# Long attention on one core: two score halves issued in turns, value column halves alternating, PSUM banks reassigned

## What is computed

```python
q = q.reshape(B, S, G, R, dh).transpose(0, 2, 3, 1, 4) * dh ** -0.5      # G=4 groups, R=4 heads each, dh=64
sc = jnp.where(vis, jnp.einsum('bgrqd,bgnd->bgrqn', qb, k_cmp), NEG)     # 15 compressed keys
o_cmp = jnp.einsum('bgrqn,bgnd->bgrqd', p_cmp, v_cmp)
sc = jnp.einsum('bgrqd,bgqkd->bgrqk', qb, ksel)                          # selected keys, causal
o_slc = jnp.einsum('bgrqk,bgqkd->bgrqd', jax.nn.softmax(sc, axis=-1), vsel)
sc = jnp.where(wmask, jnp.einsum('bgrqd,bgkd->bgrqk', qb, kwin), NEG)    # window keys, causal
o_win = jnp.einsum('bgrqk,bgkd->bgrqd', jax.nn.softmax(sc, axis=-1), vwin)
return gb[..., 0:1] * o_cmp + gb[..., 1:2] * o_slc + gb[..., 2:3] * o_win
```

## Time and profile before

| | us |
|---|---|
| median of 3 runs | 1858.64 (1858.28 to 1859.43) |
| the profiled execution, its own time | 1860.6 |
| its span, first to last instruction | 1858.7 |
| TensorE busy in it | 1715.8 (92%) |
| VectorE busy | 1038.0 (56%) |
| ScalarE busy | 791.7 (43%) |
| mean granted TensorE clock | 0.954 of full |

### The profile page before, as it was taken

One profiled execution on the slowest core, in us unless ns is written; L12 is line 12 of the kernel. 1 busy time (PEld: TensorE's weight loads), 2 busy tenths in 40 slices (PEclk: granted clock), 3 DMA queues, 4 the chain that ended last, 5 costly groups with the idle time before them and its releaser, 6 DMA issues.

```text
span 1858.7 us, 22342 instructions
## 1 busy us (share of the span) xinstructions
PE 1715.8 (92%) x8605; PEld 1414.5 (76%) x8605; DVE 1038.0 (56%) x1326; ACT 791.7 (43%) x963; POOL 96.7 (5%) x143
## 2 busy tenths in 40 slices
PE   6999978899999999989898989999899887789996
PEld 6788867688888788889855777888688673668885
DVE  4577654466655676645554435555548653655553
ACT  4434433365434444333455335555444433334441
POOL 1000000010000000010000003000100010200000
PEclk8999989999999999999899999999899895799998
DMA  8687734177864677633400425556365330536550
GB/s 288 201 277 262 233 108 157 40 255 252 268 226 147 229 259 262 225 104 101 167 33 1 139 69 174 190 189 213 108 231 204 109 106 1 170 125 203 181 181 23
DMA packets 210195, 311.74 MB, mean 168 GB/s; under 512 B 16537, under 2 KB 145589, under 8 KB 209872
## 3 DMA queue, kind: packets, MB, share of 16 engines
q1 hardware_dynamic: 204112, 288.90, 46.6%
q0 software_dynamic: 6016, 21.94, 3.4%
HBM read 306.59 MB, written 4.21 MB: 167 GB/s over the span
## 4 chain that ended last, share of the span: by engine, by line
PE 85%; DVE 6%; ACT 3%; issue 3%; DMA 1%; PEld 1%; POOL 1%; DVEq 0%; PEldq 0%; ACTq 0%; SPq 0%; POOLq 0%
PE ps L1994 24%; PE ps L1996 24%; PE ps L1995 24%; DVE wlo L1304 1%; PE ps L2035 1%; PE ps L2330 1%; PE ps L2116 1%; PE ps L2217 1%; PE ps L2315 1%; DMA area<-in_gate_b 1%; PE ps L2045 1%; PE ps L2198 1%; PE ps L2418 1%; PE ps L2306 1%; ACT xn L811 0%
## 5 line engine op out<-in xcount | busy, mean ns | idle before, releaser
L1304 DVE TENSOR_TENSOR wlo<-raw,whi 128x2048 fp32r<-128x2048 f32 x255 | 581.0, 2298 | 238.1 <-ACT whi L757 237.3
L757 ACT ACTIVATE whi<-raw 128x2048 fp32r<-128x2048 f32 x255 | 481.2, 1910 | 207.1 <-PE ps L1996 183.7
L1994 PE MATMUL ps<-wlo,aT_hi 128*128 128x512 f32 (+1 forms) x1280 | 500.2, 391 | 22.1 <-DVE aT_lo L1330 9.2
L1996 PE MATMUL ps<-whi,aT_hi 128*128 128x512 f32 (+1 forms) x1280 | 493.4, 385 | 0.0
L1995 PE MATMUL ps<-whi,aT_lo 128*128 128x512 f32 (+1 forms) x1280 | 493.0, 385 | 0.0
L1994 PEld LDWEIGHTS ps<-wlo,aT_hi 128*128 128x128 f32 x1280 | 244.1, 191 | 72.6 <-issue 15.0
L1996 PEld LDWEIGHTS ps<-whi,aT_hi 128*128 128x128 f32 x1280 | 243.5, 190 | 47.9
L1995 PEld LDWEIGHTS ps<-whi,aT_lo 128*128 128x128 f32 x1280 | 244.2, 191 | 45.1
L1994 PE MATMUL ps<-wlo,hT_hi 128*128 128x512 f32 x480 | 188.0, 392 | 5.4 <-DVE hT_lo L1421 3.0
L1996 PE MATMUL ps<-whi,hT_hi 128*128 128x512 f32 x480 | 187.6, 391 | 0.0
L1995 PE MATMUL ps<-whi,hT_lo 128*128 128x512 f32 x480 | 187.3, 390 | 0.0
(11 more groups left out here) (302 smaller groups left out, 1388.4 us busy)
## 6 DMA issues: line engine op xcount, KB each, us to landing
raw<-in_ffn_w_in SPq DMA_DIRECT2D x176, 512.0 KB, 4.9
raw<-in_ffn_w_out SPq DMA_DIRECT2D x88, 512.0 KB, 4.3
raw<-in_w_ff SPq DMA_DIRECT2D x64, 512.0 KB, 4.7
raw<-in_ada_w SPq DMA_DIRECT2D x48, 512.0 KB, 5.5
raw<-in_w_in SPq DMA_DIRECT2D x48, 512.0 KB, 4.7
raw<-in_xattn_w_kv SPq DMA_DIRECT2D x32, 512.0 KB, 7.0
raw<-in_xattn_w_q SPq DMA_DIRECT2D x16, 512.0 KB, 4.8
raw<-in_xattn_w_o SPq DMA_DIRECT2D x16, 512.0 KB, 4.9
```

The costliest lines, as they stand in the source:

```text
L757: act.activation(to, of, ACT.Copy).then_inc(hi_ready[slot], 1)
L1304: dve.tensor_tensor(lo, of, hi, ALU.subtract).then_inc(lo_ready[slot], 1)
L1994: pe.matmul(o, lh, rl, start=start, stop=False, skip_group_check=True)
L1996: return pe.matmul(o, lh, rh, start=False, stop=stop, skip_group_check=True)
```

## The change

Only `nsa_attend` is edited, on all three engines for the bank numbers, and on TensorE for the order.

- Scores of two units (an even and an odd head) are issued as one `score_pair(p)`: selected keys of the even head, selected keys of the odd head, window keys of the even head, window keys of the odd head. They use four banks (u % 4) instead of three.
- `values(gi)` issues both column halves in one step, alternating half 0 and half 1 for each stationary operand, between turn(4 gi + 4) and turn(4 gi + 5). Both halves accumulate in bank 7, which alone serves all groups; so it waits for out_lo of the group directly before, not of the one before that.
- Turned probabilities move to banks 4 and 5, turn_cmp to bank 6. turn_cmp is issued after the fourth unit of a group rather than after the third.
- The score of units 2p + 4 and 2p + 5 is issued after turn(2p + 1).

The numbers of matmuls, transposes, copies and vector instructions, and their shapes, are unchanged. The core of the diff:

```diff
-                    def score(u):
-                        g, t, r = u // 8, u // 4 % 2, u % 4
-                        half, w = slice(64 * (r % 2), 64 * (r % 2) + 64), P * (t + 1)
-                        if u >= 3:
-                            pe.wait_ge(maxed, units.n + u - 2)
-                        q = qT[half, 2 * g + r // 2, t * P:(t + 1) * P]
-                        pe.matmul(ps[:, u % 3, 0:w], q, ksT[half, g, 0:w], start=True, stop=True)
-                        pe.matmul(ps[:, u % 3, w:2 * w], q, kwT[half, g, 0:w], start=True, stop=True).then_inc(scored, 1)
+                    def score_pair(p):
+                        g, t, k = p // 4, p // 2 % 2, p % 2
+                        w = P * (t + 1)
+                        if p >= 2:
+                            pe.wait_ge(maxed, units.n + 2 * p - 2)
+                        for c, keys in ((0, ksT), (w, kwT)):
+                            for e in range(2):
+                                half = slice(64 * e, 64 * e + 64)
+                                last = pe.matmul(ps[:, (2 * p + e) % 4, c:c + w], qT[half, 2 * g + k, t * P:(t + 1) * P],
+                                                 keys[half, g, 0:w], start=True, stop=True)
+                                if c:
+                                    last.then_inc(scored, 1)
...
-                    def values(gi, half):
+                    def values(gi):
...
-                        if gi >= 2:
-                            pe.wait_ge(o_kept, groups.n + gi - 1)
-                        o = ps[64 * half:64 * half + 64, 6 + gi % 2, 0:256]
-                        pe.matmul(o, vcmp[:, 64 * g:64 * g + 64], nsaPc[gi % 2][0:N_CMP, half::2, :], start=True, stop=False)
+                        if gi:
+                            pe.wait_ge(o_kept, groups.n + gi)
+                        terms = [(vcmp[:, 64 * g:64 * g + 64], nsaPc[gi % 2][0:N_CMP])]
                         for j, v in enumerate((vs, vw)):
                             for m in range(t + 1):
                                 c = P * (j * (t + 1) + m)
-                                last = pe.matmul(o, v[:, m, 64 * g:64 * g + 64], nsaP[gi % 2][:, half::2, c:c + P],
-                                                 start=False, stop=j == 1 and m == t)
-                        if half == 1:
-                            last.then_inc(pv_done, 1)
+                                terms.append((v[:, m, 64 * g:64 * g + 64], nsaP[gi % 2][:, :, c:c + P]))
+                        for n, (v, probs) in enumerate(terms):
+                            for half in range(2):
+                                last = pe.matmul(ps[64 * half:64 * half + 64, 7, 0:256], v, probs[:, half::2, :],
+                                                 start=n == 0, stop=n == len(terms) - 1, skip_group_check=True)
+                        last.then_inc(pv_done, 1)
...
-                    score(0)
-                    score(1)
-                    keep_clock(30, 5)
-                    for u in range(32):
-                        if u + 2 < 32:
-                            score(u + 2)
-                        turn(u)
-                        if u % 4 == 2:
-                            turn_cmp(u // 4)
-                        if u % 4 < 2 and u >= 4:
-                            values(u // 4 - 1, u % 4)
-                    for half in range(2):
-                        values(7, half)
+                    score_pair(0)
+                    score_pair(1)
+                    keep_clock(30, 4)
+                    for p in range(16):
+                        turn(2 * p)
+                        if p % 2 == 0 and p:
+                            values(p // 2 - 1)
+                        turn(2 * p + 1)
+                        if p % 2:
+                            turn_cmp(p // 2)
+                        if p + 2 < 16:
+                            score_pair(p + 2)
+                    values(7)
```

More of the change, by code:

```diff
@@ L1036, in keep @@
                             act.wait_ge(pv_done, groups.n + gi - 1)
-                        act.activation(nsaP[gi % 2][:, r, 0:2 * P * (t + 1)], ps[:, 3 + u % 2, 0:2 * P * (t + 1)], ACT.Copy)\
+                        act.activation(nsaP[gi % 2][:, r, 0:2 * P * (t + 1)], ps[:, 4 + u % 2, 0:2 * P * (t + 1)], ACT.Copy)\
                            .then_inc(probs_kept, 1)
@@ L1043, in out_hi @@
                         act.activation(aT_hi[:, 2 * g:2 * g + 2, t * P:(t + 1) * P],
-                                       ps[:, 6 + gi % 2, 0:256].rearrange("p (j q) -> p j q", j=2), ACT.Copy).then_inc(o_hi, 1)
+                                       ps[:, 7, 0:256].rearrange("p (j q) -> p j q", j=2), ACT.Copy).then_inc(o_hi, 1)
                     def keep_cmp(gi):
@@ L1049, in keep_cmp @@
                             act.wait_ge(pv_done, groups.n + gi - 1)
-                        act.activation(nsaPc[gi % 2][0:N_CMP], ps[0:N_CMP, 5, :].rearrange("p (r q) -> p r q", r=4), ACT.Copy)\
+                        act.activation(nsaPc[gi % 2][0:N_CMP], ps[0:N_CMP, 6, :].rearrange("p (r q) -> p r q", r=4), ACT.Copy)\
                            .then_inc(cmp_kept, 1)
@@ L1639, in top @@
                         for j in range(2):
-                            last = dve.tensor_tensor_reduce(Pb[u % 3][:, w * j:w * j + w], ps[:, u % 3, w * j:w * j + w],
+                            last = dve.tensor_tensor_reduce(Pb[u % 3][:, w * j:w * j + w], ps[:, u % 4, w * j:w * j + w],
                                                             cst[:, C_CAUSAL + S - w:C_CAUSAL + S], -1.0, BIG, ALU.add, ALU.min,
@@ L1659, in out_lo @@
                         at = (slice(None), slice(2 * g, 2 * g + 2), slice(t * P, (t + 1) * P))
-                        dve.tensor_tensor(aT_lo[at], ps[:, 6 + gi % 2, 0:256].rearrange("p (j q) -> p j q", j=2),
+                        dve.tensor_tensor(aT_lo[at], ps[:, 7, 0:256].rearrange("p (j q) -> p j q", j=2),
                                           aT_hi[at], ALU.subtract).then_inc(o_kept, 1)
@@ L2314, in turn @@
                         for m in range(2 * (t + 1)):
-                            last = pe.transpose(ps[:, 3 + u % 2, P * m:P * m + P], Pb[u % 3][:, P * m:P * m + P], ident)
+                            last = pe.transpose(ps[:, 4 + u % 2, P * m:P * m + P], Pb[u % 3][:, P * m:P * m + P], ident)
                         last.then_inc(probs_turned, 1)
-                    def values(gi, half):
+                    def values(gi):
                         g, t = gi // 2, gi % 2
@@ L2340, in turn_cmp @@
                         for r in range(4):
-                            last = pe.transpose(ps[0:N_CMP, 5, P * r:P * r + P], cmpP[:, t, 4 * g + r, :], ident)
+                            last = pe.transpose(ps[0:N_CMP, 6, P * r:P * r + P], cmpP[:, t, 4 * g + r, :], ident)
                         last.then_inc(cmp_turned, 1)
```

## The result

The changed kernel takes 1867.61 us (median of 5 runs, 1862.74 to 1870.45) beside 1859.38 us for the kernel before: a ratio of 1.0034, 95% interval 1.0021 to 1.0048. It is slower by 0.2 to 0.5%, where a gain of 2.3 us was forecast. The profiled execution took 1862.74 us (span 1860.8), the fastest of the five and 2.1 us more than the profiled execution of before.

What follows compares the result with a forecast made beforehand. TensorE was taken to bound nine tenths of `nsa_attend`, a chain of waits the rest. Full-clock 74.4 us becomes 87.9 with 0.53 at half clock, plus 1 for `project`: 88.9 against 91.2, so 1858.64 - 2.3 = 1856.3 us; range 1844 to 1868.

Steps and rivals of the forecast that it cites:

- Overlap of halves: Scores and values in nsa_attend: a pair costs one unit (0.64 or 1.06 us), both value halves cost one (1.58 or 2.45).
- D: Values in nsa_attend: column halves accumulating in one bank do not overlap, row halves do; stage 93.4 us, total 1861; chance 0.07.
- E: Scores and values in nsa_attend: nothing overlaps; stage 100.2 us, total 1868; chance 0.05.
- Chain and cover: After turn(5): the 3.43 us chain to turn(6) stays, its cover goes; TensorE idles 2.8 us instead of 1.14.
- Lengths at full clock: nsa_attend: lead-in about 5.8 us, pattern of eight units 18.6, tail 12.8, stage 74.4, 16.8 less than before.
- The clock falls and returns, half of the time low: TensorE in nsa_attend: the clock falls in nearly every group and returns; share of stage at half clock 0.53.
- B: nsa_attend: the clock mostly holds; share at half clock 0.1 gives 1844 us, 0 gives 1841.8; chance 0.22.
- rival C: nsa_attend: the clock falls and stays down; share 0.9 gives 1870 us, slower above share 0.60; chance 0.17.
- The price of half clock: nsa_attend: a pattern wholly at half clock takes 26.2 us against 18.6, so the stage is 74.4 / (1 - 0.29 x).
- rival A: nsa_attend, the forecast itself: halves overlap, clock falls and returns, share 0.35 to 0.7; 1851 to 1862 us; chance 0.49.
- The next stage: `project`, after nsa_attend: sometimes starts at half clock, costing 1 us more.
- The subtraction of 2.0 us: Whole program: the profiled execution of the kernel before was 2.0 us above its median, taken over for the forecast.

Runs made afterwards that it cites:

- the one before with its output later: The kernel before with out_hi one unit later on ScalarE and out_lo two units later on VectorE: 1863.59 us, ratio 1.0031.
- The second profile: The changed kernel run once more, unedited, to profile another of its executions: 1866.91 us, ratio 1.0030.
- the kernel with nothing in turns and the fill: The changed kernel with neither scores nor values alternating, plus unread matmuls ahead of the third and fourth units' turns: 1860.51 us, ratio 0.9996.
- the values in sequence: The changed kernel with the values' column halves one after the other, scores still in pairs: 1878.09 us, ratio 1.0091.
- the values in the chain: The changed kernel with values(gi) issued after turn(4 gi + 5) instead of ahead of it: 1855.28 us, ratio 0.9960.
- the first fill of the changed kernel: The changed kernel with 76 unread matmuls added on TensorE ahead of the turns of each group's third and fourth units: 1845.15 us, ratio 0.9916.
- the kernel before with its clock held: The kernel before with 4 (large group) or 2 (small) unread matmuls added ahead of the third unit's turn: 1856.65 us, ratio 0.9978.

## Why the prediction was wrong, point by point

- **Overlap of halves: right.** Values 1.60 and 2.46 for both halves (forecast 1.58 and 2.45), pairs 0.65 and 1.07 (0.64 and 1.06). The estimate of a quarter more, worked out from the figure for three column tiles in the Trainium skill (TensorE: Matmul & The Clock Gate, section "Measured speedup vs the span model"), is not borne out for two halves: at full clock no loss can be seen. Rivals D and E fall. But the scores need no alternation, only that two units follow each other.
- **Chain and cover: right.** TensorE idle 2.59 ahead of turn(6), forecast 2.8; the wait of out_lo is 31.7 in all, forecast "some 20": the chain is there, its total was under-sized.
- **Lengths at full clock: right.** With the clock held: lead-in 5.87 (5.8), pattern 18.4 (18.6), tail 13.05 (12.8), stage 74.18 (74.4).
- **The clock falls and returns, half of the time low: right.** Half of the stage at 1.2 GHz (forecast 0.53). There were eight falls, one in each group, and all but the last ended within the stage. So rivals B and C did not occur here; C's mechanism showed in one kernel, the one before with its output later. The Trainium skill (same page, section "HAM oscillation — how this bites in real kernels") describes a kernel that waits 3 to 5 us for a transfer in each turn of its loop and starts each turn at the low clock. The trace agrees in kind, with waits of 2.59 us and less, and for other engines instead of transfers.
- **The price of half clock: wrong, and this turned the sign.** The prediction took 0.29 us lost per us at half clock. It came from a pattern wholly at half clock, with its 4.0 us of waits in it, which lose nothing. The traces have 0.36 to 0.39. The falls are not spread over the pattern: the idle time passes at full clock (967.58 to 970.24 at 1.00) and the low clock covers the dense turns, values and pairs behind it (971.20 to 981.20, busy 9.69 of 10; over all eight falls 42.3 of 46.6), which take 1.8 to 1.9 times as long. Rows 1 and 9 had it: the fall in the kernel before lasted 6.80 us, all of them busy, and cost 2.95, 0.43 a microsecond. With 0.39 the same share x = 0.53 gives 74.4 / (1 - 0.21) = 93.8 instead of 87.9, 2.6 us more than before rather than 3.3 less. The point from which it is slower, by the prediction's own sum with 1 us for `project`, falls from x = 0.60 to about 0.45, so what was rival C's territory was the middle of rival A.
- **The next stage: under-sized.** 1 us was put down for `project` at half clock; it was 2.1, since the last fall, behind a wait of 3.2 us in the tail, went on to 1032.
- **Together:** with the measured share 0.50, 0.39 and 2.1 the sum is 74.4 / (1 - 0.195) + 2.1 = 94.5 against 91.2, 1863.9 for the profiled execution; it took 1862.74.
- **The runs around the profile.** The subtraction of 2.0 us to reach the median was taken over from before. In the changed kernel the profiled execution was the fastest, and the median lies 4.9 us above it. The second profile puts part of its excess in the stage and part outside, and leaves the rest open: the slower executions have mean clocks of 0.939 to 0.946 over the span beside 0.946 in the fastest, but none of the slowest was profiled. Of the 11.3 us between the forecast of 1856.3 and the median, 4.4 lie between the profiled execution and the sum for it (1858.3), 2.0 are the subtraction and 4.9 the excess of the median. The price and `project` explain the first; the cause of the excess stays open. The time stayed within the range of 1844 to 1868, at its edge.

## What to carry to other kernels

Price a fall of TensorE's clock by the work that it covers, not by a mean over a pattern: falls come behind the waits and lie on the dense part, so each microsecond at half clock cost 0.36 to 0.39 us here and 0.43 in the kernel before, where a mean over a pattern gave 0.29. Where overlap shortens TensorE's work and leaves the chain that it waits for, look at once for what the wait does to the clock; moving the chain's blocking step (here out_lo ahead of weigh) was worth 29 us, and some matmuls for nobody in the waits 22. Put a change behind a held clock before judging its parts: the values' overlap was worth 15 us at full clock and some 10 without the held clock, and that the pairs' turns are worth nothing could be read only with it.

## What the runs showed of the hardware that was not expected

- Two row halves overlap when issued one after the other (0.65 us for a pair, as in turns). The column halves, whose runs are longer, do so only in turns (2.46 against 4.89 us, 953.41 to 958.30 in the kernel with nothing in turns and the fill).
- Overlap of two is complete in float32: 16 value matmul records in 1.95 us, where 8 take 1.94.
- A fall does not need a long wait: one came 1.3 us after a wait of 0.63 us and lasted some 51 us of busy time in which single halves ran. In the changed kernel seven of eight falls ended after 3.4 to 10.2 us. Whether work in two halves at once is what brings the clock back stays open: with the values in sequence falls ended too (mean clock 0.79), and why the long one lasted was not settled.
- Where the clock is left to the waits, executions can differ much: 7.7 us from fastest to slowest in the changed kernel, 9.8 with the values in the chain, 24.5 with the kernel before and its output later, against 4.1 with the first fill of the changed kernel. It is no rule: the second batch of the changed kernel differs by 2.3 only, and the kernel before with its clock held by 6.2.
